# A fused decoder block on one core: the ways into and out of the seven-product down projection

## The chip, the core and the metric

One Trainium2 chip, one core. The time is that of one execution on the device, in microseconds; a measurement is the median of several runs.

## The reference, cut to what matters

The kernel computes one decoder block on 2048 tokens of width 1024 in float32: an input projection, two kinds of mixers, an output projection, and a SwiGLU feed-forward of width 2816. The change touches only the end of it:

```
u = rmsnorm(h, ln2_g)
h = h + (silu(u @ w_gate) * (u @ w_up)) @ w_down
out = rmsnorm(h, final_g)
```

## The kernel before

**Number format.** Every float32 matmul is made of three: each operand is split into a high part (a copy by ScalarE, type fp32r) and a low part (raw minus high, by the vector engine), and high x high, high x low and low x high are added in a PSUM bank.

**Seven products.** The feed-forward works on pairs of 512-token blocks, p = 0 and 1 (`NPAIR` = 2). Each 2 x 2 block product is done as seven products of sums of blocks in place of eight (Strassen's way, in Winograd's form). In the gate and up stage the operands made from u are `B11, B21, T2, T1, T3, B22, T4`, each 128 x 2048, and the weights `A11, A12, S2, S1, S3, S4, A22`, in that order, for `NG` = 22 groups (even groups are gate, odd ones up; `NJ` = 11 pairs of groups). A product is 12 matmuls of 128x512. In `ffn(p)` the vector engine combines and multiplies into `au[0..3]` (the four blocks of the activated result) and then makes three sums of them, in `gq[1..3]`: `s1 = au2 + au1` (line 2050), `s2 = s1 - au0` (2052), `s4 = au3 - s2` (2062). SyncE (SP), which issues all DMAs in program order, stores the four blocks (`store_a`, line 629) and the three sums (`store_s`, 634) to a scratch in HBM. `gq[0..3]` also hold the gate's results before that: the last readers are lines 2024, 2038, 2048 and 2058.

**The down projection.** `down(p)` has 7 products of `NJ` = 11 rows, `NR` = 77 ring rows. A ring row is 128 x 1024: one half from `w_down` or its combined form `t_scr`, one half from the stored blocks (`load_row`, lines 668 and 675). It goes through a ring of `CRING` = 4 slots; the slot of row rr is free when row rr-4 is done (`s_row`). ScalarE splits high (`row_hi`, 1566), the vector engine low (`row_lo`, 2110), each two rows ahead in its program, and TensorE does 12 matmuls (1165 to 1167). Ring slot 3 lies on `gq`: its high part on gq[0] and gq[1], its raw and low part on gq[2] and gq[3]. So `load_row` for rr = 3 waits until all sums are stored (`s_sst >= 48 * NJ * (p + 1)`), and it is called only at the start of SP's `down(p)`, behind all stores of the last group; rows 0 to 2 are loaded within the last group of `ffn(p)`.

**What goes on beside the rows.** After each product the vector engine adds the four banks to the residual (`residual`, 2123), one per row at the first four rows of the next product. ScalarE sums the squares of finished halves (`out_square`, 1576; it waits for the residual add); for the last of them before the end it does so at product 6, rows j = 0 to 3, that is ring rows 66 to 69, behind `row_hi` of two rows ahead. Then come `out_sums` (2130), `out_root` (1583, with a table load), `out_rn` (2134), four `out_scale` (2139) at j = 5 to 8, and the stores of the outputs (`store_out`, 693; the first is waited for before the rest is issued). The second half of a pair's outputs follows after the last row: in pair 0 within the next gate stage, in pair 1 at the very end. The third and fourth weight block of the next gate stage wait for one and for four of these stores (lines 1500 and 1502), as their buffers held residuals.

**Preparing the next pair in down(0).** The operand pieces of pair 1 and the residual pieces are loaded one beside each ring row by the list `PIECES` (operands by name, `("r", n)` residuals), from row 4 on. `COMBINE_AT` gives the rows at which the vector engine makes T3, T1, T2, T4 (`combine`, 1959), `SPLIT_AT` the rows of the operand splits: `op_hi` (1481) on ScalarE one row earlier, `op_lo` (1991) on the vector engine. Counting semaphores (`s_ophi`, `s_oplo`) assume an order, so far that of the operand numbers.

**Combined weights.** In `ffn(0)` the combined down weights are made: `load_t(j)` (642) from group `T_LOAD` = 10 on, `t_step` (2095 to 2105, four adds) one group later, `store_t(j)` (647) two groups later, 1 MB each way, in the two buffers `tw`; the last is stored after the last group. The buffers were `h_last` before, so the first load waits for the store of u (`store_u`).

Of the kernel before, what the change touches and what calls it, by code (L numbers as in the profile page):

```python
# [40 lines left out]
P = 128  # L41
# [38 lines left out]
OPERAND_NAMES = {"B11": B11, "B21": B21, "T2": T2, "T1": T1, "T3": T3, "B22": B22, "T4": T4}  # L80
KH = 4
# [8 lines left out]
PIECES = (("r", 0), "T3", "T1", ("r", 2), "T2", ("r", 1), "T4", "B11", "B21", ("r", 3), "B22")  # L90
COMBINE_AT = {27: 0, 38: 1, 41: 2, 49: 3}
SPLIT_AT = {51: "B11", 54: "B21", 59: "T2", 61: "T1", 63: "T3", 70: "B22", 75: "T4"}
T_LOAD = 10
# [37 lines left out]
def block_program(nc, x, ln1_g, w_in, lb_logits, hgrn_norm_g, attn_sinks, attn_norm_g, w_out, ln2_g,  # L131
# [37 lines left out]
    with ExitStack() as ctx:  # L169
# [153 lines left out]
        dump = acc_last  # L323
        tw = [at(f"tw{i}", (P, 2, D), kk_at + 8 * K * i) for i in range(2)]

# [223 lines left out]
        def _(sp):  # L549
# [81 lines left out]
            def store_s(p, j, n):  # L631

                sp.wait_ge(s_au, 7 * (p * NJ + j) + (4, 5, 7)[n])
                sp.dma_start(a_scr[p, (3, 2, 5)[n], j, :, :], gq[1 + n][:, :]).then_inc(s_sst, 16)
# [14 lines left out]
            def load_row(p, rr):  # L649
# [12 lines left out]
                elif rr == 3:  # L662
                    sp.wait_ge(s_sst, 48 * NJ * (p + 1))
# [13 lines left out]
            def load_res(p, m, b, half):  # L677
                if half == m == 0 and b == 0:
# [5 lines left out]
                    if p:  # L684
                        sp.wait_ge(s_fo, 32 * TB * p)
                it = 2 * p + m
# [48 lines left out]
            def ffn(p):  # L735
# [5 lines left out]
                for g in range(NG):  # L741
                    j = g // 2
                    if p == 0 and g >= T_LOAD + 2:
# [6 lines left out]
                    else:  # L750
# [9 lines left out]
                        if last:  # L760
                            load_row(p, 1)
                            load_row(p, 2)
                        store_s(p, j, 0)
# [4 lines left out]
                    if p == 0 and g == 9:  # L768
                        store_u(NSB - 1, 0)
                        store_u(NSB - 1, 1)  # L770
                if p == 0:
                    store_t(NJ - 1)

            def down(p):
# [3 lines left out]
                for rr in range(3, NR):  # L778
# [47 lines left out]
        def _(pe):  # L826
# [280 lines left out]
            def ffn_product(p, g, o):  # L1107
# [6 lines left out]
                if g == 0:  # L1114
                    pe.wait_ge(s_oplo, PRODUCTS * p + o + 1)
# [76 lines left out]
        def _(act):  # L1192
# [392 lines left out]
            def down(p):  # L1585
                for rr in range(NR):
# [7 lines left out]
                    if q == 6 and j < TB:  # L1594
                        out_square(p, 2 * TB + j)
                    if q == 6 and j == TB + 1:
# [37 lines left out]
        def _(dve):  # L1634
# [350 lines left out]
            def op_lo(p, o):  # L1985

                dve.wait_ge(s_ophi, PRODUCTS * p + o + 1)
# [15 lines left out]
            def ffn(p):  # L2003
                for g in range(NG):
# [3 lines left out]
                    for o in range(PRODUCTS):  # L2008
# [30 lines left out]
                        if o == S4:  # L2039
# [5 lines left out]
                            if up:  # L2045
# [4 lines left out]
                                V.tensor_tensor(gq[1][:, :], au[2][:, :], au[1][:, :], ALU.add).then_inc(s_au, 1)  # L2050
                                dve.wait_ge(s_au, 7 * j + 4)
                                V.tensor_tensor(gq[2][:, :], gq[1][:, :], au[0][:, :], ALU.subtract).then_inc(s_au, 1)
                        if o == A22 and up:
# [8 lines left out]
                            V.tensor_tensor(gq[3][:, :], au[3][:, :], gq[2][:, :], ALU.subtract).then_inc(s_au, 1)  # L2062
# [79 lines left out]
            def down(p):  # L2142
                for rr in range(NR):
# [5 lines left out]
                    if q == 6 and j == TB:  # L2149
# [193 lines left out]
```

## Time and profile before

| | us |
|---|---|
| median of 3 runs | 2281.8 |
| lowest, highest | 2279.1, 2285.85 |
| profiled execution, its own time | 2285.81 |
| its span, first to last instruction | 2284.0 |
| TensorE busy | 2222.6 (97%) |
| vector engine busy | 1438.3 (63%) |
| ScalarE busy | 1010.2 (44%) |
| GpSimd busy | 443.8 (19%) |

The profiled execution is a single one, 4 us above the median. Engines: PE is TensorE's matmuls, DVE the vector engine, ACT ScalarE, POOL GpSimd, SPq the queue of SyncE, which issues the DMAs. Starts are in us from the span's start. A bracket at the end of a row gives the idle time of that engine just before the instruction and what released it. TensorE's granted clock is told as a share of full speed: 1.00 is 2.4 GHz, 0.50 is 1.2 GHz. The first `ffn` ends at 1408 us, `down(0)` lasts to 1632 us, the second `ffn` to 2053 us.

### The profile page before, as it was taken

The numbers are of one execution on the slowest core, as the hardware profiler recorded it, in microseconds if no ns is written. First come the engines' busy times: TensorE is split into PE (matmuls) and PEld (weight loads), VectorE is DVE, ScalarE is ACT, GpSimd is POOL, SyncE is SP. The second block draws the span as 40 slices with busy tenths as digits, with TensorE's granted clock in tenths as the row PEclk, the third lists the DMA queues.
The fourth block names the chain that finished last, engine by engine and source line by source line (L and its number), as shares of the span: only waits on it lengthen the run. The fifth ranks groups of instructions, "written<-read, shape, count | busy, mean of one in ns | idle before, by whom it ended". The sixth has DMA issues, their size and how long they took to land.

```text
span 2284.0 us, 29991 instructions
## 1 busy us (share of the span) xinstructions
PE 2222.6 (97%) x11144; PEld 1848.9 (81%) x11144; DVE 1438.3 (63%) x2170; ACT 1010.2 (44%) x1723; POOL 443.8 (19%) x344
## 2 busy tenths in 40 slices
PE   7999999999999999999999999999999999999997
PEld 6888878887888788878888887888788888887886
DVE  5775568656865677675566666467665555554555
ACT  5554455445554554444433333345533333333444
POOL 2231022201220122032233331000232222210000
PEclk9999999999999999999999999999999999999999
DMA  4222333233233313533345656788443232326765
GB/s 122 92 75 80 115 102 96 90 107 105 81 121 97 111 58 119 194 105 117 116 164 183 223 205 216 255 269 262 149 137 108 99 109 98 110 89 213 229 221 197
DMA packets 260705, 321.80 MB, mean 141 GB/s; under 512 B 17233, under 2 KB 168785, under 8 KB 259537
## 3 DMA queue, kind: packets, MB, share of 16 engines
q1 hardware_dynamic: 258256, 311.50, 41.5%
q10 hardware_dynamic: 2304, 8.39, 0.9%
q8 instruction: 89, 1.46, 0.3%
q14 instruction: 56, 0.45, 0.1%
HBM read 242.76 MB, written 77.07 MB: 140 GB/s over the span
## 4 chain that ended last, share of the span: by engine, by line
PE 86%; DVE 5%; issue 3%; ACT 3%; DMA 2%; POOL 0%; SPq 0%; ACTq 0%; DVEq 0%; POOLq 0%
PE M L1138 9%; PE M L1140 9%; PE M L1139 9%; PE M L831 7%; PE M L833 7%; PE M L832 7%; PE M L1165 3%; PE M L1167 3%; PE M L1166 3%; PE X L1165 3%; PE X L1166 3%; PE X L1167 3%; PE X L1140 3%; PE X L1139 3%; PE X L1138 3%
## 5 line engine op out<-in xcount | busy, mean ns | idle before, releaser
L2110 DVE TENSOR_TENSOR ring_lo<-ring_raw,ring_hi 128x1024 fp32r<-128x1024 f32 x154 | 189.4, 1230 | 186.9 <-ACT ring_hi L1566 186.5
L1663 DVE TENSOR_TENSOR wlo<-raw,whi 128x1024 fp32r<-128x1024 f32 x120 | 152.0, 1267 | 230.3 <-ACT whi L1201 230.1
L831 PE MATMUL M<-uhi,whi 128*128 128x512 f32 (+1 forms) x720 | 286.4, 398 | 3.7 <-DVE wlo L1663 2.1
L833 PE MATMUL M<-uhi,wlo 128*128 128x512 f32 (+1 forms) x720 | 278.7, 387 | 0.0
L832 PE MATMUL M<-ulo,whi 128*128 128x512 f32 (+1 forms) x720 | 278.1, 386 | 0.0
L1566 ACT ACTIVATE ring_hi<-ring_raw 128x1024 fp32r<-128x1024 f32 x154 | 162.8, 1059 | 239.4 <-DMA ring_raw<-a_scr 236.2
L1138 PE MATMUL M<-t_hi,wu_hi 128*128 128x512 f32 x616 | 240.8, 391 | 4.1 <-DVE gq L2032 2.3
L1140 PE MATMUL M<-t_hi,wu_lo 128*128 128x512 f32 x616 | 240.6, 391 | 0.0
L1139 PE MATMUL M<-t_lo,wu_hi 128*128 128x512 f32 x616 | 240.4, 390 | 0.0
L1201 ACT ACTIVATE whi<-raw 128x1024 fp32r<-128x1024 f32 x120 | 126.6, 1055 | 196.9 <-PE M L833 146.2
L2000 DVE TENSOR_TENSOR wu_lo<-fraw,wu_hi 128x512 fp32r<-128x512 f32 x132 | 127.5, 974 | 120.3 <-ACT wu_hi L1507 120.0
L2254 POOL TENSOR_TENSOR pr<-pr,rd 128x512 f32<-128x512 f32 x64 | 84.4, 1318 | 539.7 <-DVE rd L1696 539.7
L831 PEld LDWEIGHTS M<-uhi,whi 128*128 128x128 f32 x720 | 136.9, 190 | 32.3 <-issue 4.2
L833 PEld LDWEIGHTS M<-uhi,wlo 128*128 128x128 f32 x720 | 136.4, 189 | 27.9
L2306 POOL TENSOR_TENSOR fs<-fraw 128x512 f32<-128x512 f32 x44 | 64.8, 1474 | 481.1 <-DMA fraw<-in_w_gate_dram 214.9
L832 PEld LDWEIGHTS M<-ulo,whi 128*128 128x128 f32 x720 | 137.1, 190 | 24.3
L1138 PEld LDWEIGHTS M<-t_hi,wu_hi 128*128 128x128 f32 x616 | 115.9, 188 | 29.8 <-DVE wu_lo L2000 5.6
L1165 PE MATMUL M<-ring_hi 128*128 128x512 f32 x308 | 123.1, 400 | 15.4 <-DVE ring_lo L2110 15.4
L1139 PEld LDWEIGHTS M<-t_lo,wu_hi 128*128 128x128 f32 x616 | 116.1, 188 | 24.1
L1140 PEld LDWEIGHTS M<-t_hi,wu_lo 128*128 128x128 f32 x616 | 116.0, 188 | 24.1
L2312 POOL TENSOR_TENSOR fraw<-fraw,fs 128x512 f32<-128x512 f32 x44 | 57.4, 1305 | 372.1 <-DVE wl_lo L2000 372.0
L1277 ACT ACTIVATE pr<-pr,nm 128x256 f32<-128x256 f32 x128 | 64.2, 502 | 145.0 <-DVE nms L1722 145.0
(277 smaller groups left out, 5109.3 us busy)
## 6 DMA issues: line engine op xcount, KB each, us to landing
raw<-in_w_in_dram SPq DMA_DIRECT2D x88, 512.0 KB, 3.8
ring_raw<-a_scr SPq DMA_DIRECT2D x154, 256.0 KB, 3.6
fraw<-in_w_gate_dram SPq DMA_DIRECT2D x44, 512.0 KB, 4.6
fraw<-in_w_up_dram SPq DMA_DIRECT2D x44, 512.0 KB, 4.8
a_scr<-au SPq DMA_DIRECT2D x88, 256.0 KB, 2.3
ring_raw<-t_scr SPq DMA_DIRECT2D x88, 256.0 KB, 3.0
a_scr<-gq SPq DMA_DIRECT2D x66, 256.0 KB, 2.5
ring_raw<-in_w_down_dram SPq DMA_DIRECT2D x66, 256.0 KB, 3.0
```

The source lines that it names most:

```text
L831: mm(bank, whi[s][:, kb, :], hi, start=first, stop=False)
L832: mm(bank, whi[s][:, kb, :], lo, start=False, stop=False)
L833: return mm(bank, wlo[s][:, kb, :], hi, start=False, stop=last)
L1138: mm(bank[:, :], wh[:, k, :], hi[:, k, :], start=start and k == 0, stop=False, skip_group_check=True)
L1139: mm(bank[:, :], wh[:, k, :], lo[:, k, :], start=False, stop=False, skip_group_check=True)
L1140: last = mm(bank[:, :], wl[:, k, :], hi[:, k, :], start=False, stop=k == KH - 1, skip_group_check=True)
L1165: mm(banks[b][:, :], hi[:, 1, tokens], hi[:, 0, :], start=first, stop=False, skip_group_check=True)
L1166: mm(banks[b][:, :], hi[:, 1, tokens], lo[:, 0, :], start=False, stop=False, skip_group_check=True)
L1167: done = mm(banks[b][:, :], lo[:, 1, tokens], hi[:, 0, :], start=False, stop=last, skip_group_check=True)
L1566: A(hi[:, :, :], raw_r[:, :, :], ACT.Copy).then_inc(s_rowhi, 1)
L1663: V.tensor_tensor(wlo[s][:, :, :], raw[s][:, :, :], whi[s][:, :, :].bitcast(F32), ALU.subtract).then_inc(s_lo[s], 1)
L2110: V.tensor_tensor(lo[:, :, :], raw_r[:, :, :], hi[:, :, :].bitcast(F32), ALU.subtract).then_inc(s_rowlo, 1)
```

## The change

Four edits, all in the second half of the kernel.

1. The sums of the last group of each `ffn(p)` go to three buffers of their own, `sx`, which lie on the second `tw` buffer (and on parts of the second half's residuals). The vector engine waits before the first of them: in pair 0 for the store of combined weights 9, in pair 1 for all outputs of pair 0. `load_row` for rr = 3 moves into the last group, ahead of the stores of the sums, and waits for the last reader of gq (`s_c21[1]`) and for the sums of the groups before. The wait for all sums moves to the first residual load of the second half.
2. In `down(p)` the squares of product 6 come at j = 2 to 5 in place of 0 to 3, and what follows from them two rows later: `out_sums` at j = 6, `out_root` and `out_rn` at 7, the scalings at 7 to 10.
3. The operands are split in another order, all of them by row 65, and B22's pieces are loaded before the last residual's. `SPLIT_ORDER` gives the counters the place of each operand.
4. `T_LOAD` is 9 in place of 10, the last `store_t` goes to the start of group 21, and the store of u goes to the end of group 8.

```diff
+SPLIT_ORDER = (tuple(range(PRODUCTS)), (B11, T2, T1, T3, B21, T4, B22))
-PIECES = (("r", 0), "T3", "T1", ("r", 2), "T2", ("r", 1), "T4", "B11", "B21", ("r", 3), "B22")
-COMBINE_AT = {27: 0, 38: 1, 41: 2, 49: 3}
-SPLIT_AT = {51: "B11", 54: "B21", 59: "T2", 61: "T1", 63: "T3", 70: "B22", 75: "T4"}
-T_LOAD = 10
+PIECES = (("r", 0), "T3", "T1", ("r", 2), "T2", ("r", 1), "T4", "B11", "B21", "B22", ("r", 3))
+COMBINE_AT = {27: 0, 37: 1, 39: 2, 48: 3}
+SPLIT_AT = {50: "B11", 52: "T2", 54: "T1", 59: "T3", 61: "B21", 63: "T4", 65: "B22"}
+T_LOAD = 9
...
+        sx = [at(f"sx{i}", (P, T), kk_at + 8 * K + 2 * K * i) for i in range(3)]
+        def sums_of(j):
+            return sx if j == NJ - 1 else gq[1:4]
...
-                sp.dma_start(a_scr[p, (3, 2, 5)[n], j, :, :], gq[1 + n][:, :]).then_inc(s_sst, 16)
+                sp.dma_start(a_scr[p, (3, 2, 5)[n], j, :, :], sums_of(j)[n][:, :]).then_inc(s_sst, 16)
...
                 elif rr == 3:
-                    sp.wait_ge(s_sst, 48 * NJ * (p + 1))
+                    sp.wait_ge(s_c21[1], NJ * (p + 1))
+                    sp.wait_ge(s_sst, 48 * (NJ * (p + 1) - 1))
...
+                if m and b == 0:
+                    sp.wait_ge(s_sst, 48 * NJ * (p + 1))
...
-                    if p == 0 and g >= T_LOAD + 2:
+                    if p == 0 and 0 <= g - T_LOAD - 2 < NJ:
                         store_t(g - T_LOAD - 2)
...
                             load_row(p, 1)
                             load_row(p, 2)
+                            load_row(p, 3)
                         store_s(p, j, 0)
...
-                    if p == 0 and g == 9:
+                    if p == 0 and g == T_LOAD - 1:
                         store_u(NSB - 1, 0)
                         store_u(NSB - 1, 1)
-                if p == 0:
-                    store_t(NJ - 1)
...
-                for rr in range(3, NR):
+                for rr in range(CRING, NR):
                     load_row(p, rr)
...
-                    pe.wait_ge(s_oplo, PRODUCTS * p + o + 1)
+                    pe.wait_ge(s_oplo, PRODUCTS * p + SPLIT_ORDER[p].index(o) + 1)
...
-                    if q == 6 and j < TB:
-                        out_square(p, 2 * TB + j)
-                    if q == 6 and j == TB + 1:
+                    if q == 6 and 2 <= j < 2 + TB:
+                        out_square(p, 2 * TB + j - 2)
+                    if q == 6 and j == TB + 3:
                         out_root(p, 0)
...
-                dve.wait_ge(s_ophi, PRODUCTS * p + o + 1)
+                dve.wait_ge(s_ophi, PRODUCTS * p + SPLIT_ORDER[p].index(o) + 1)
...
-                                V.tensor_tensor(gq[1][:, :], au[2][:, :], au[1][:, :], ALU.add).then_inc(s_au, 1)
+                                if g == NG - 1 and p:
+                                    dve.wait_ge(s_fo, 32 * TB * p)
+                                elif g == NG - 1:
+                                    dve.wait_ge(s_ts, 16 * (NJ - 1))
+                                s1, s2, _ = sums_of(g // 2)
+                                V.tensor_tensor(s1[:, :], au[2][:, :], au[1][:, :], ALU.add).then_inc(s_au, 1)
                                 dve.wait_ge(s_au, 7 * j + 4)
-                                V.tensor_tensor(gq[2][:, :], gq[1][:, :], au[0][:, :], ALU.subtract).then_inc(s_au, 1)
+                                V.tensor_tensor(s2[:, :], s1[:, :], au[0][:, :], ALU.subtract).then_inc(s_au, 1)
...
-                            V.tensor_tensor(gq[3][:, :], au[3][:, :], gq[2][:, :], ALU.subtract).then_inc(s_au, 1)
+                            _, s2, s4 = sums_of(g // 2)
+                            V.tensor_tensor(s4[:, :], au[3][:, :], s2[:, :], ALU.subtract).then_inc(s_au, 1)
...
-                    if q == 6 and j == TB:
+                    if q == 6 and j == TB + 2:
                         out_sums(p, 0)
-                    if q == 6 and j == TB + 1:
+                    if q == 6 and j == TB + 3:
                         out_rn(p, 0)
-                    if q == 6 and 0 <= j - TB - 1 < TB:
-                        out_scale(p, 0, j - TB - 1)
+                    if q == 6 and 0 <= j - TB - 3 < TB:
+                        out_scale(p, 0, j - TB - 3)
```

## Rows read from the trace of the kernel before

**Rows 1.** The page: engine totals, instruction groups, DMA issues (last column: us to landing).

```profile
PE 2222.6 (97%) x11144; PEld 1848.9 (81%) x11144; DVE 1438.3 (63%) x2170; ACT 1010.2 (44%) x1723; POOL 443.8 (19%) x344
...
L2110 DVE TENSOR_TENSOR ring_lo<-ring_raw,ring_hi 128x1024 fp32r<-128x1024 f32 x154 | 189.4, 1230 | 186.9 <-ACT ring_hi L1566 186.5
...
L1165 PE MATMUL M<-ring_hi 128*128 128x512 f32 x308 | 123.1, 400 | 15.4 <-DVE ring_lo L2110 15.4
...
ring_raw<-a_scr SPq DMA_DIRECT2D x154, 256.0 KB, 3.6
```

**Rows 2.** Stretches: length, busy us of five engines, clock, DMA share, GB/s.

```profile
1420.00:1422.00 2.00, 0.35 (x1) 0.35 (x2) 1.56 (x2) 1.39 (x2) 0.00 (x0) 0.50 0.99 354
1500.00:1600.00 100.00, 100.00 (x440) 82.03 (x439) 69.50 (x58) 52.19 (x58) 0.00 (x0) 1.00 0.82 265
```

**Rows 3.** Timeline of TensorE: rows 0, 1, 3, 4 of down(0), and its successor.

```profile
1408.07 0.39 PE L1165 MATMUL M<-ring_hi 128*128 128x512 f32 x1
...
1411.50 0.50 PE L1165 MATMUL M<-ring_hi 128*128 128x512 f32 x1 [0.55 <-DVE ring_lo L2110]
...
1421.65 0.79 PE L1165 MATMUL M<-ring_hi 128*128 128x512 f32 x1 [4.38 <-DVE ring_lo L2110]
...
1426.70 0.39 PE L1165 MATMUL M<-ring_hi 128*128 128x512 f32 x1
...
1632.36 0.39 PE L1138 MATMUL M<-b_hi,wl_hi 128*128 128x512 f32 x1
```

**Rows 4.** Timeline of SyncE's queue, way into down(0): last sum's store, row 3's load.

```profile
1410.59 0.43 SPq L634 DMA_DIRECT2D a_scr<-gq  x1
...
1414.27 0.33 SPq L668 DMA_DIRECT2D ring_raw<-in_w_down_dram  x1
```

**Rows 5.** Timeline of TensorE: rows 0, 3 and 4 of down(1).

```profile
2053.13 0.39 PE L1165 MATMUL M<-ring_hi 128*128 128x512 f32 x1
...
2067.33 0.80 PE L1165 MATMUL M<-ring_hi 128*128 128x512 f32 x1 [5.03 <-DVE ring_lo L2110]
...
2072.13 0.39 PE L1165 MATMUL M<-ring_hi 128*128 128x512 f32 x1
```

**Rows 6.** Timelines of three engines, way into down(1): row 2's load and split.

```profile
2051.70 0.43 SPq L675 DMA_DIRECT2D ring_raw<-a_scr  x1
...
2053.39 0.68 DVE L2058 TENSOR_TENSOR au<-M,gq 128x512 f32<-128x512 f32 x1
...
2056.92 1.06 ACT L1566 ACTIVATE ring_hi<-ring_raw 128x1024 fp32r<-128x1024 f32 x1 [2.16 <-DMA ring_raw<-a_scr]
```

**Rows 7.** Timeline of TensorE: rows 69 to 72 of down(0).

```profile
1604.09 0.39 PE L1165 MATMUL M<-ring_hi 128*128 128x512 f32 x1
...
1608.08 0.50 PE L1165 MATMUL M<-ring_hi 128*128 128x512 f32 x1 [1.10 <-DVE ring_lo L2110]
...
1611.64 0.50 PE L1165 MATMUL M<-ring_hi 128*128 128x512 f32 x1 [0.51 <-DVE ring_lo L2110]
...
1616.99 0.50 PE L1165 MATMUL M<-ring_hi 128*128 128x512 f32 x1 [2.30 <-DVE ring_lo L2110]
```

**Rows 8.** Timelines of the vector engine and ScalarE at the same place.

```profile
1605.88 2.14 DVE L2110 TENSOR_TENSOR ring_lo<-ring_raw,ring_hi 128x1024 fp32r<-128x1024 f32 x1 [1.74 <-ACT ring_hi L1566]
...
1608.65 0.63 ACT L1576 ACTIVATE acc_last<-res 128x512 f32<-128x512 f32 x1 [2.81 <-DVE res L2123]
...
1612.84 1.90 ACT L1481 ACTIVATE b_hi<-b_raw 128x2048 fp32r<-128x2048 f32 x1
```

**Rows 9.** Waits of TensorE, 2230 to 2284 us: total, times, longest.

```profile
PE M L1165 <- DVE ring_lo L2110: 1.1, 2, 0.6
```

**Rows 10.** Tail of down(1): timeline of the vector engine; waits of SyncE's queue, 2236 to 2284 us.

```profile
2268.53 1.28 DVE L2139 SCALAR_TENSOR_TENSOR res<-res,rnrm,gfrow 128x1024 f32<-128x1024 f32 x1
2270.95 0.69 DVE L2123 TENSOR_TENSOR res<-res,M 128x512 f32<-128x512 f32 x1 [1.14 <-PE M L1167]
...
SPq L693 <- DMA out_dram<-res: 3.4, 1, 3.4
```

## The prediction

> **What bounds the kernel now.** I read the page first. TensorE is busy 2222.6 us [rows 1] of a span of 2284.0, so at most 61.4 us of idle time can go, and the busy part only where its clock was down. The page's largest idle sum in front of a matmul of the second half is 15.4 us, before line 1165, the down projection, and its releaser is the vector engine's low split of a ring row (line 2110). Then the table of stretches [rows 2]: in mid-stream the down projection has TensorE busy 100% at the full granted clock (1.00, the 2.4 GHz level), and at 1420 to 1422 us it is almost idle at 0.50, the 1.2 GHz level. So the loss sits where a down projection begins and ends, and I read those places in order of time.
>
> A ring row is 12 matmuls. Undisturbed, row starts are 2.72 us apart, so 77 rows would take 209.5 us. The first down projection takes 1408.07 to 1632.36 [rows 3] = 224.3 us, 14.8 us more.
>
> **Way in, first pair.** Row 1 starts at 1411.50 where 1410.79 was due (1408.07 + 2.72): 0.7 us late, and the clock stays up. Rows 1 and 2 take it to 1416.94, but row 3 starts at 1421.65, 4.7 us late, and row 4 comes 5.05 us later in place of 2.72, since the clock is down: 2.3 us more [rows 3]. Why is row 3 late? SyncE (SP) issues the first of its two loads at 1414.27, having waited for the last store of a sum (line 634, issued at 1410.59) to land, and only then can the row travel and be split [rows 4]. Its buffer, ring slot 3, is the memory of gq, whose sums are being stored.
>
> **Way in, second pair.** The same: row 0 starts at 2053.13, row 3 at 2067.33 with 5.03 us idle before it, so it was due at about 2062.15 (an end of a matmul reaches 0.16 us past the next start), and row 4 at 2072.13 [rows 5]. That is 5.2 us of waiting and 2.1 us of low clock.
>
> **Part 1, sums apart and row 3 loaded in advance.** The three sums of the last group go to sx. What slot 3 then waits for is the multiply of line 2058, the last reader of gq[3], begun at 2053.39 and 0.68 us long [rows 6]. So the pair is issued at about 2054.15 and 2054.6 instead of behind the landed stores. The time of such a load from the second issue to landing has a median of 3.6 us on the page [rows 1]; row 2 of this pair, issued at 2051.70 and taken by ScalarE at 2056.92, needed 5.2 us [rows 6]. High and low split take 1.06 us [rows 6] and 1.23 us [rows 1], with hand-overs 2.35 us. Row 3 is then ready between 2060.6 and 2062.2, and due at 2062.15: 0 to 0.1 us late. I take 0. In the first pair line 2058 lies equally far behind the start of row 0, so the same holds.
>
> What it pushes back: row 3's two loads now stand on SP ahead of the five remaining stores, which go out some 1.3 us later than before. Nobody reads them before row 22, 60 us later, and the residual loads behind them have as long. Behind the stores comes row 4: five issues of 0.43 us [rows 4] with their gaps take some 2.3 us (2055.1 to 2057.4), then its own pair, second issue 2057.8, landing after 3.6 to 5.2 us, ready 2063.8 to 2065.4, due 2064.87: 0 to 0.5 us late. I take 0.3 us for each way in; a delay that short left the clock up at 1411.50 [rows 3]. The Trainium skill ("DMA: Bandwidth & Descriptors", section on queues, rings and completion order) says that an engine's semaphore increment lands only after every earlier write of that engine. By it row 3 would be independent of the stores behind it and row 4 would wait out the 1.25 MB ahead of it. No row shows the two apart; by it the sum would keep row 3 at 0 and put row 4 at its late end, 0.4 us less gain in all.
>
> The vector engine's new waits ask for stores finished long before (combined weights of step 9, a whole group earlier; the first pair's outputs): 0. If step 9's store were still under way, the wait would hold the rest of the last group. The early load gains 4.7 + 2.3 + 5.2 + 2.1 = 14.3 us, less 0.6 = 13.7.
>
> **Part 2, way out: squares two rows later.** In the first pair row starts go 1604.09, 1608.08, 1611.64, 1616.99 [rows 7], the end being 1632.36 [rows 3]. Eight rows are 21.8 us; they take 28.3: 6.5 us lost. ScalarE's square waits for the residual add, the add stands behind the vector engine's low split, and that stands behind ScalarE's high split, which is queued behind the previous square: at 1608.65 ScalarE had been idle 2.81 us for a residual [rows 8]. High split, low split, residual, square make a ring of 3.56 us a row (1608.08 to 1611.64) against 2.72. Then at 1612.84 comes the 1.90 us split of B22 on ScalarE, and the next row is 2.6 us late with 1.8 us of low clock behind it. Two rows later every square finds its residual done, so the ring opens; B22 goes to row 65. In the second pair there is no B22: two waits for a low split, 1.1 us together [rows 9], that is two rows of 3.56 us, 1.7 us lost.
>
> I take all of it back, 8.2 us. One delay in it has another cause: the low split at 1605.88 took 2.14 us instead of 1.23 [rows 8] while GpSimd was making sums, and that stays. Outside the ring a row has three rows' time, 8.2 us, from the release of its slot: less 0.8 for two issues, 3.6 for landing and 2.35 for the splits that leaves 1.4 us, so 0.9 more is covered; if it is not, 0 to 1 us stays. Nothing excludes that.
>
> **Part 3, splits in another order.** The same seven ScalarE splits (1.90 us, as at 1612.84) and seven vector splits, none added. Rows 59 to 63 keep every second place; row 65 takes the fourth. ScalarE then has 1.0 + 1.9 us in a 2.72 us row once, and less in the next. Each operand's last piece is loaded at least three rows before its split. 0, with 0 to 1 us for the range. SP issues no DMA more; B22's pieces and the last residual's change places.
>
> **Part 4, T_LOAD a step earlier.** The 1 MB load and store of each step move one group forward. The last group of the first pair loses four vector adds of 0.68 us, which lie in front of its sums: row 1 comes up to 0.1 us sooner. The 1 MB store also leaves SP at 1411, where it preceded row 3. The two u stores wait on SP before group 9 instead of 10; what is behind them is not due for a group. 0.
>
> **Part 5, what gets later: outputs.** The scalings of the first half of a pair's outputs move to rows 73 to 76. In the last pair they now run up against the residual adds after the last row. The last scaling began at 2268.53, right behind the low split of row 76 (1.14 us from start to start, so 2267.4), the first add at 2270.95, and ScalarE's four squares and the end follow that add [rows 10]. With the split at 2267.1 to 2267.4 and three scalings of 1.22 us behind it, the add begins at 2271.9 to 2272.2: **1.0 us lost**, between 0.9 and 1.3. After the first pair the third and fourth weight blocks of the next gate stage wait for those outputs to be stored (lines 1500, 1502). Four stores, the first alone and waited for 3.4 us [rows 10], are down 3.6 us after the last row; block four must be on ScalarE by 6.8 us after it (three products of 2.72 less two splits). 0, with 3 us of slack.
>
> **Sum.** 13.7 + 8.2 - 1.0 = 20.9, less 0.5 for small delays of the unbounded kind above = 20.4 us. The profiled execution took 2285.8 us (span 2284.0), so 2265.4 by its own time; the median shown, 2281.8, is 4.0 lower, so I predict 2281.8 - 20.4 = **2261.4 us**.
>
> **Rivals.** (A) The wait on row 3 is replaced by one on DMA: rows 3 and 4 stay late by 1 to 2 us each way in and the clock falls once more. Row 2's 5.2 us speaks for it [rows 6], the 2.7 us of stores and the free row ahead against. It keeps about 3 us for each way in: gain 14.4, 2267.4. Chance 0.16. (B) The way out is bound by loads or by GpSimd's sharing and not by the ring, so half of the 8.2 stays, or the fourth split in a row costs it again: gain 16 with a part of A, down to 13, about 2267. The 2.14 us split speaks for it, the idle 2.81 us with releaser "residual" against. Chance 0.12. (C) Slower: the output stores come so late that ScalarE stands at line 1502 and TensorE starves at the fourth product. Each us beyond 6.8 costs one; it turns the sign only when they land 24 us later than I work out (3.2 slack and 20.4 gain), then 2285 or more. Four stores of 3.4 us one after another, from 5 us before the last row's end, would be down 8.6 us after it and cost 1.8. Chance 0.02. (D) The change does not do what it says: row 3 still waits for a landed store (of the group before) or the squares still meet a fresh residual. The waits' counts speak against; gain under 8, 2276. Chance 0.03.
>
> **Numbers.** Forecast 0.67. Its own range is 2257 to 2265: no more than the 22.5 us found can go, runs scatter by 3 us. To hold 8 in 10 with A and B the upper end goes to 2270. 0.3%, 6.8 us, is what a measurement can tell from no change: faster 0.95, same 0.03, slower 0.02.
>
> **What would show it.** Row 3 of each pair starting within 0.5 us of 2.72 us after row 2 at clock 1.00, ScalarE's wait before it under 3 us, no row start over 2.9 us apart in the last ten rows, first add of the tail 1 us closer to the last matmul. Wrong if TensorE's time in a down projection stays above 215 us, if a gap appears at the fourth product of the second gate stage, or a new one near rows 50 to 65.

## The result, and the profile after

| | before | after |
|---|---|---|
| median of 5 runs, us | 2284.6 | 2268.6 |
| lowest, highest | 2279.1, 2285.85 | 2267.18, 2272.28 |
| profiled execution | 2285.81 | 2272.28 |
| its span | 2284.0 | 2270.6 |
| first down projection, row 0 to the next stage | 224.3 | 214.2 |
| second down projection, row 0 to its last matmul's end* | 219.6 | 214.8 |
| last matmul's end to the end of the span | 11.3 | 12.3 |

(*) The end of a matmul is taken here as its start plus 0.23 us, the distance of two matmuls at full clock.

The ratio after to before is 0.9937 (0.9923 to 0.9951): faster by 14 us, the medians differ by 16. The median lies 7.2 us above the forecast of 2261.4, outside the forecast's own range of 2257 to 2265 and inside the one that was widened to 2270 for the rivals. Two thirds to four fifths of the forecast gain of 20.4 us came. The kernel before has a median of 2284.6 over five runs, where the forecast started from 2281.8 over three; set on the same base the forecast would have been 2264.2, and the miss 4.4 us.

The page of the kernel after (the lines that answer to [rows 1]; line numbers moved, 1165 is 1174, 2110 is 2125):

```profile
PE 2217.9 (98%) x11144; PEld 1847.1 (81%) x11144; DVE 1437.9 (63%) x2170; ACT 1010.0 (44%) x1723; POOL 445.8 (20%) x344
...
L1174 PE MATMUL M<-ring_hi 128*128 128x512 f32 x308 | 120.7, 392 | 6.1 <-DVE ring_lo L2125 6.1
```

Idle time in front of the down projection's matmuls fell from 15.4 to 6.1 us, and some busy time went too, since less of it ran at the low clock. What is left is in the ways in. Timeline of TensorE, both ways in of the kernel after (start, length, engine, line, operation):

```profile
1408.57 0.39 PE L1174 MATMUL M<-ring_hi 128*128 128x512 f32 x1
...
1411.90 0.50 PE L1174 MATMUL M<-ring_hi 128*128 128x512 f32 x1 [0.45 <-DVE ring_lo L2125]
...
1422.28 0.50 PE L1174 MATMUL M<-ring_hi 128*128 128x512 f32 x1 [1.90 <-DVE ring_lo L2125]
...
2043.50 0.39 PE L1174 MATMUL M<-ring_hi 128*128 128x512 f32 x1
...
2052.57 0.50 PE L1174 MATMUL M<-ring_hi 128*128 128x512 f32 x1
...
2058.02 0.50 PE L1174 MATMUL M<-ring_hi 128*128 128x512 f32 x1 [2.44 <-DVE ring_lo L2125]
2058.89 0.63 PE L1174 MATMUL X<-ring_hi 128*128 128x512 f32 x1
```

Row 3 starts at 2052.57 without a wait: where [rows 5] had 5.03 us of idle time there is 0.1 us of delay. But the next row, row 4, waits, 1.90 us in the first pair (2.1 us late, start to start) and 2.44 us in the second (2.7 us late), and there the clock falls once more: seven matmuls behind it start 0.43 us apart in place of 0.23. The wait has moved by one row and is about half as long.

Why row 4 is late, from SyncE's queue and from ScalarE in the second pair. Line 675 loads the weight half of a row, 682 the activation half, 640 and 635 are the stores of sums and blocks:

```profile
2044.47 0.33 SPq L675 DMA_DIRECT2D ring_raw<-in_w_down_dram  x1
2044.85 0.43 SPq L682 DMA_DIRECT2D ring_raw<-a_scr  x1
2045.33 0.90 SPq L640 DMA_DIRECT2D a_scr<-sx  x2
2046.27 1.66 SPq L635 DMA_DIRECT2D a_scr<-au  x2
2047.98 0.60 SPq L640 DMA_DIRECT2D a_scr<-sx  x1
2048.63 0.60 SPq L675 DMA_DIRECT2D ring_raw<-in_w_down_dram  x1
2049.27 0.67 SPq L682 DMA_DIRECT2D ring_raw<-a_scr  x1
```

```profile
2050.19 1.06 ACT L1575 ACTIVATE ring_hi<-ring_raw 128x1024 fp32r<-128x1024 f32 x1 [2.52 <-DMA ring_raw<-a_scr]
2055.65 1.06 ACT L1575 ACTIVATE ring_hi<-ring_raw 128x1024 fp32r<-128x1024 f32 x1 [4.40 <-DMA ring_raw<-a_scr]
```

Row 3 is issued at 2044.47, as soon as the last reader of gq (line 2058 before, 2072 now) is done, and is with ScalarE 5.3 us after its second issue. Behind it go the five stores. Their issues stretch (two of them take 1.66 us where one takes 0.43), so row 4's second issue is at 2049.27, 5.8 us after row 0's start instead of the 4.7 I had; and the row is with ScalarE 6.4 us later, where I had allowed 3.6 to 5.2. In the first pair the same two numbers are 5.6 and 5.7 us. Stretches of the same time (length, busy us of five engines, clock, DMA share, GB/s):

```profile
2044.00:2048.00 4.00, 3.55 (x16) 2.62 (x15) 3.07 (x5) 2.12 (x2) 0.00 (x0) 1.00 0.74 235
2048.00:2052.00 4.00, 4.00 (x20) 3.27 (x18) 1.65 (x2) 1.06 (x1) 0.00 (x0) 1.00 1.05 362
2052.00:2056.00 4.00, 3.58 (x15) 2.36 (x13) 0.51 (x1) 0.35 (x1) 0.00 (x0) 1.00 1.00 345
```

From 2048 to 2056 the 16 DMA engines are busy all the time (mean share 1.00 to 1.05). I read this as transfers that wait for their turn behind other bytes, and not for their own latency; the stretches alone do not show it.

The way out is clean. ScalarE at the place of [rows 8]: every square (1585) stands directly behind a high split (1575) and waits for nothing, and what the high splits wait for is their load:

```profile
1602.34 1.06 ACT L1575 ACTIVATE ring_hi<-ring_raw 128x1024 fp32r<-128x1024 f32 x1 [1.31 <-DMA ring_raw<-a_scr]
1603.30 0.61 ACT L1585 ACTIVATE acc_last<-res 128x512 f32<-128x512 f32 x1
...
1605.11 1.06 ACT L1575 ACTIVATE ring_hi<-ring_raw 128x1024 fp32r<-128x1024 f32 x1 [1.10 <-DMA ring_raw<-a_scr]
1606.07 0.62 ACT L1585 ACTIVATE acc_last<-res 128x512 f32<-128x512 f32 x1
```

A slow low split that runs beside GpSimd's sums is there still, 1.85 us at 1603.43 in place of 1.23, and costs nothing (that GpSimd is what slows it was not tested):

```profile
1603.43 1.85 DVE L2125 TENSOR_TENSOR ring_lo<-ring_raw,ring_hi 128x1024 fp32r<-128x1024 f32 x1 [1.16 <-ACT ring_hi L1575]
```

The tail pays for it. Vector engine after the last low split, where [rows 10] had 1.14 us of idle time before the first add:

```profile
2253.86 3.67 DVE L2154 SCALAR_TENSOR_TENSOR res<-res,rnrm,gfrow 128x1024 f32<-128x1024 f32 x3
2257.45 0.68 DVE L2138 TENSOR_TENSOR res<-res,M 128x512 f32<-128x512 f32 x1
```

The last matmul ends at 2258.33; the first add begins 0.9 us before that, where it began 1.8 us before it.

### The profile page after: what moved, and what is told of

It is laid out like the page before. It is cut to its first block, busy times and chain, and to the rows that moved or that the text cites. A ratio compares the mean times of both kernels' runs of the same rounds, so it can differ in the third digit from the quotient of the medians.

```text
span 2270.6 us, 29999 instructions
## 1 busy us (share of the span) xinstructions
PE 2217.9 (98%) x11144; PEld 1847.1 (81%) x11144; DVE 1437.9 (63%) x2170; ACT 1010.0 (44%) x1723; POOL 445.8 (20%) x344
## 4 chain that ended last, share of the span: by engine, by line
PE 87%; DVE 5%; issue 3%; ACT 2%; DMA 2%; SPq 0%; POOL 0%; ACTq 0%; DVEq 0%; POOLq 0%
PE M L1147 9%; PE M L1149 9%; PE M L1148 9%; PE M L840 7%; PE M L842 7%; PE M L841 7%; PE M L1174 3%; PE M L1176 3%; PE M L1175 3%; PE X L1149 3%; PE X L1147 3%; PE X L1148 3%; PE X L1175 3%; PE X L1174 3%; PE X L1176 3%
```

## The experiments

Eleven measurements, each set against the kernel before on the same chip: nine new kernels, one of them twice, and the changed kernel once more. Two theories of the late row 4: **S**, it waits out what stands ahead of it in SyncE's queue (the five stores, 1.25 MB); **R**, it shares the DMA engines with what is issued behind it. "Down 1" and "down 2" are the two down projections in the profiled execution, measured as in the table above, "row 4" the idle time of TensorE before that row, "tail" the time from the last matmul's end to the end of the span.

| kernel | median us | ratio to before, 95% | down 1, down 2 | row 4, both pairs | tail |
|---|---|---|---|---|---|
| after | 2268.6 | 0.9937 (0.9923, 0.9951) | 214.2, 214.8 | 1.90, 2.44 | 12.3 |
| changed_again | 2268.8 | 0.9933 (0.9920, 0.9946) | 213.4, 212.2 | 2.25, 1.59 | 12.2 |
| stores_beside_rows | 2261.4 | 0.9904 (0.9887, 0.9921) | 211.5, 210.7 | none | 12.3 |
| stores_beside_again | 2262.9 | 0.9905 (0.9890, 0.9920) | 212.5, 211.4 | none | 12.2 |
| residual_loads_later | 2268.1 | 0.9931 (0.9914, 0.9947) | 213.5, 212.4 | 1.47, 1.40 | 12.3 |
| stores_behind_row4 | 2268.2 | 0.9924 (0.9910, 0.9938) | 212.8, 212.3 | none (row 5: 1.41, 1.50) | 12.2 |
| t_load_back | 2269.1 | 0.9932 (0.9918, 0.9946) | 216.7, 212.7 | 3.81, 1.93 | 12.2 |
| squares_back | 2271.5 | 0.9949 (0.9934, 0.9964) | 216.3, 214.7 | 1.37, 2.33 | 11.4 |
| split_order_back | 2268.1 | 0.9934 (0.9920, 0.9949) | 214.6, 212.6 | 2.24, 1.96 | 12.3 |
| squares_alone | 2276.0 | 0.9958 (0.9945, 0.9972) | 219.3, 218.3 | row 3: 4.83, 4.99 | 12.1 |
| stores_tail | 2264.4 | 0.9910 (0.9896, 0.9924) | 211.6, 211.0 | none | 11.4 |
| stores_in_free_rows | 2262.4 | 0.9906 (0.9892, 0.9921) | 211.8, 210.2 | none | 11.4 |

**stores_beside_rows.** The stores leave the space between rows 3 and 4:

```diff
                         if last:
                             load_row(p, 3)
-                        store_s(p, j, 0)
-                        store_s(p, j, 1)
-                        store_a(p, j, 2)
-                        store_a(p, j, 3)
-                        store_s(p, j, 2)
+                        if not last:
+                            for n in range(5):
+                                store_rest(p, j, n)
...
                     load_row(p, rr)
+                    if rr in (5, 6, 7, 8, 9):
+                        for n in range(5):
+                            if (5, 6, 7, 8, 9)[n] == rr:
+                                store_rest(p, NJ - 1, n)
```

(`store_rest` issues the five in the old order.)

> The changed kernel, with the five stores that stand on SyncE between the loads of row 3 and row 4 issued one by one beside rows 5 to 9 instead. In the changed kernel's profile row 3 was in time in both ways in, and row 4 was the late one (1.9 and 2.4 us idle before it, once with the clock down behind it); its down projections took 214.2 and 214.8 us. Theory S (row 4 waits out the 1.25 MB of stores ahead of it in the queue): row 4 starts less than 0.3 us late in both, the clock stays at 1.00, the projections take about 212 and 210.5 us, and the time falls by 4 to 6 us against the changed kernel, to about 0.9915 of the kernel before. Theory R (row 4 shares the engines with the residual pieces and rows 5 and 6 behind it): row 4 stays 1.5 to 2.5 us late, no change of time beyond 1 us.

Row 4 has no wait in either pair, no projection is over 211.5 us, and the median is 7 us lower than the changed kernel's in the table at the top (5.9 us where the two were measured side by side, see below). This is theory S as written, at the upper end of the 4 to 6 us expected or a little above. Its queue (row 4) and ScalarE (rows 3 and 4) in the second pair, where row 0 starts at 2038.69:

```profile
2041.61 0.33 SPq L680 DMA_DIRECT2D ring_raw<-in_w_down_dram  x1
2041.99 0.47 SPq L687 DMA_DIRECT2D ring_raw<-a_scr  x1
```

```profile
2044.36 1.06 ACT L1582 ACTIVATE ring_hi<-ring_raw 128x1024 fp32r<-128x1024 f32 x1 [1.73 <-DMA ring_raw<-a_scr]
2046.25 1.06 ACT L1582 ACTIVATE ring_hi<-ring_raw 128x1024 fp32r<-128x1024 f32 x1 [0.82 <-DMA ring_raw<-a_scr]
```

Two things improve together: the second issue is 3.3 us after row 0's start instead of 5.8, and the row is with ScalarE 4.3 us later instead of 6.4. The two shares, 2.5 us of later issue and 2.1 us of longer travel, are about equal. Row 3 gains too: without the five stores behind it it is with ScalarE 4.3 us after its second issue, where it took 5.3 us with them in the kernel after. Over the profiles of all kernels that load row 3 in advance it is 3.8 to 4.8 us without the stores directly behind row 3 and 4.9 to 5.6 us with them. So stores behind a load do delay it, by about 0.9 us on average; row 3 has just that much to spare.

**residual_loads_later.** The pieces of residual 0, beside rows 4, 5, 6 and 8, go beside rows 7 to 10:

```diff
+                for rr in (4, 5, 6, 8):
+                    del pieces[rr]
...
+                    if 7 <= rr < 7 + TB:
+                        load_res(p, 0, rr - 7, 0)
```

> The changed kernel, with the four pieces of the first residual (256 KB each, beside rows 4, 5, 6 and 8) loaded beside rows 7 to 10; the five stores stay where they are. Theory S (the stores ahead hold row 4): row 4 is still 1.5 us late or more in at least one way in, time within 2 us of the changed kernel. Theory R (what is issued behind row 4 holds it): row 4 less than 0.5 us late in both, and 4 to 6 us less time.

Row 4 still waits 1.47 and 1.40 us (its start is 1.8 and 1.7 us late), and the time is the same. The bound for S was a start 1.5 us late or more, so S holds, narrowly. The waits are shorter than in the two profiles of the changed kernel (1.59 to 2.44), but squares_back, whose way in is the same, has one of 1.37 us. So what is issued behind row 4 is not the cause as a whole, and a share of some tenths of a microsecond is possible but not shown here.

**stores_behind_row4.** The same bytes in another order:

```diff
                             load_row(p, 3)
+                            load_row(p, 4)
                         store_s(p, j, 0)
...
                 for rr in range(CRING, NR):
-                    load_row(p, rr)
+                    if rr > CRING:
+                        load_row(p, rr)
```

> The changed kernel with the loads of row 4 between row 3's and the five stores. SyncE then waits for row 0 to be done before the stores go out, some 2 us later than now; the same bytes, another order. Theory S: row 4 is in time in both ways in (wait under 0.3 us). The 1.25 MB are now ahead of row 5, which is issued about 7 us after row 0 begins and must land by 11.8: with 3.1 us of stores it is 0 to 1.5 us late. Time 2 to 5 us below the changed kernel. Theory R (row 4 shares with what is issued behind it): row 4 stays 1 us late or more, since the stores are then right behind it.

The sharpest of the runs. With the stores directly behind row 4 instead of ahead of it, row 4 does not wait, and row 5, which now has them ahead, does. ScalarE in the second pair (rows 4 and 5), and TensorE at row 5:

```profile
2048.62 1.06 ACT L1577 ACTIVATE ring_hi<-ring_raw 128x1024 fp32r<-128x1024 f32 x1 [0.59 <-DMA ring_raw<-a_scr]
2054.58 1.06 ACT L1577 ACTIVATE ring_hi<-ring_raw 128x1024 fp32r<-128x1024 f32 x1 [4.90 <-DMA ring_raw<-a_scr]
```

```profile
2056.95 0.50 PE L1176 MATMUL M<-ring_hi 128*128 128x512 f32 x1 [1.50 <-DVE ring_lo L2127]
```

R falls as the cause of the wait: it wanted row 4 late with the stores right behind it. Row 5 also tells in what form the stores ahead cost time: its second issue comes 8.6 and 9.1 us after row 0's start, where stores_beside_rows has 6.8, but from there it takes 5.0 and 4.5 us, against 4.7 and 4.6. Its delay is time in SyncE's program, with hardly any longer travel. For row 4 of the changed kernel, where both grew, no run separates the two. The time did not fall by the 2 to 5 us expected in the medians (2268.2), since row 5's wait took row 4's place; the ratio, 0.9924, is 0.1% lower than the changed kernel's, within the intervals.

**t_load_back.** Edit 4 undone, which puts the last 1 MB store of combined weights ahead of row 4 as well:

```diff
-T_LOAD = 9
+T_LOAD = 10
...
+                if p == 0:
+                    store_t(NJ - 1)
```

> The changed kernel with edit 4 alone undone: T_LOAD 10, and the last 1 MB store of combined weights at the start of SyncE's program for the down projection, now behind the five stores and ahead of row 4. Theory S (row 4 waits out the bytes ahead of it): 1 MB more is 2.5 us at the 410 GB/s that the stretches show, so in the first pair row 4 is 4 to 5 us late instead of 2.1 and the clock falls to 0.50 behind it (2 us more): the first down projection takes 218 to 219 us instead of 214.2, the second is unchanged at 212.5 to 215, and the time is 4 us above the changed kernel. Rival (the load of row 4 is late for its own latency, whatever is ahead): both unchanged, time the same within 1 us.

Row 4 of the first pair waits 3.81 us (4.0 us late, start to start) with low clock behind it, the second pair, where this edit changes nothing, waits 1.93 us. First pair, SyncE (the store, then row 4) and ScalarE:

```profile
1411.80 0.72 SPq L653 DMA_DIRECT2D t_scr<-tw  x1
1412.57 0.68 SPq L675 DMA_DIRECT2D ring_raw<-in_w_down_dram  x1
1413.29 1.19 SPq L682 DMA_DIRECT2D ring_raw<-a_scr  x1
```

```profile
1420.18 1.06 ACT L1576 ACTIVATE ring_hi<-ring_raw 128x1024 fp32r<-128x1024 f32 x1 [5.91 <-DMA ring_raw<-a_scr]
```

More bytes ahead, a later row: the dose goes the way S says, with 1.9 us for 1 MB rather than 2.5. The down projection takes 216.7 us, less than the 218 to 219 expected, and the median shows only 0.5 us. So edit 4 is worth some 2.5 us in the profile, which the runs' scatter does not confirm.

**squares_back.** Edit 2 undone, the rest as changed:

```diff
-                    if q == 6 and 2 <= j < 2 + TB:
-                        out_square(p, 2 * TB + j - 2)
-                    if q == 6 and j == TB + 3:
+                    if q == 6 and 0 <= j < 0 + TB:
+                        out_square(p, 2 * TB + j - 0)
+                    if q == 6 and j == TB + 1:
                         out_root(p, 0)
```

(and `out_sums`, `out_rn` and `out_scale` two rows earlier likewise)

> The changed kernel with edit 2 alone undone: the squares of product 6 at rows 66 to 69 again, sums, root and scalings two rows earlier; the order of the splits stays new. Ring theory (high split, low split, residual add and square wait for each other at 3.56 us a row): the first down projection loses 2 to 4 us near rows 69 to 72, without the 2.6 us of the B22 split, the second 1.7 us with two waits of about 0.55 us; the tail is 1.0 us shorter (11.3 us from the last matmul to the end instead of 12.3). In all 3 to 5 us slower than the changed kernel. Rival (the way out was lost to the split of B22 alone): no gap at rows 69 to 72, 1 us faster than the changed kernel by the tail.

Three waits come back in the first way out, and two of 0.51 and 0.55 us in the second. TensorE in the first:

```profile
1601.29 0.50 PE L1174 MATMUL M<-ring_hi 128*128 128x512 f32 x1 [0.90 <-DVE ring_lo L2125]
1604.85 0.50 PE L1174 MATMUL M<-ring_hi 128*128 128x512 f32 x1 [0.55 <-DVE ring_lo L2125]
1608.41 0.50 PE L1174 MATMUL M<-ring_hi 128*128 128x512 f32 x1 [0.53 <-DVE ring_lo L2125]
```

The row starts are 3.56 us apart, as in [rows 7], and ScalarE is again released by the residual add:

```profile
1597.95 0.63 ACT L1585 ACTIVATE acc_last<-res 128x512 f32<-128x512 f32 x1 [1.89 <-DVE res L2138]
1598.49 0.19 ACT L1585 ACTIVATION_READ_ACCUMULATOR acc_last<-res 128x1 f32 x1
1598.58 1.04 ACT L1575 ACTIVATE ring_hi<-ring_raw 128x1024 fp32r<-128x1024 f32 x1
```

The tail is 0.9 us shorter. The median is 2.9 us higher, at the lower end of the 3 to 5 us expected, and the intervals of the two ratios overlap: what carries this run is the profile. There the ring theory holds; the rival, that B22 alone was to blame, would have shown no gap. By row starts the ring takes 3.0 us in the first way out and 1.8 in the second. Before, the first way out lost 6.5: so B22's split, while it stood inside the ring, added some 3.5 us.

Of the clock: row 4 of the second pair waits 2.33 us here and TensorE's granted clock stays up behind it, while it fell behind the 2.30 us wait of [rows 7]. TensorE at this wait:

```profile
2057.10 0.50 PE L1174 MATMUL M<-ring_hi 128*128 128x512 f32 x1 [2.33 <-DVE ring_lo L2125]
```

The next row starts 2.85 us later, and the clock is 1.00 from 2058 to 2059. Before, it was 0.50 from 1618 to 1619, and the row took 4.45 us.

**split_order_back.** Edit 3 undone, that is `SPLIT_ORDER[1]`, `PIECES`, `COMBINE_AT` and `SPLIT_AT` as before:

```diff
-SPLIT_AT = {50: "B11", 52: "T2", 54: "T1", 59: "T3", 61: "B21", 63: "T4", 65: "B22"}
+SPLIT_AT = {51: "B11", 54: "B21", 59: "T2", 61: "T1", 63: "T3", 70: "B22", 75: "T4"}
```

> The changed kernel with edit 3 alone undone: operands split in the old order, B22 at row 70 and T4 at row 75, the last residual loaded before B22; squares stay at rows 68 to 71. Theory N (the squares' ring was what made the way out late, and the order of the splits is worth nothing by itself): at row 70 ScalarE has 1.06 + 0.82 + 1.90 us in a row of 2.72, which the lead of 1.4 us covers, so the first down projection stays within 1 us of 214.2, and the three small waits (0.24 to 0.33 us at 1550 to 1582) go: time the same within 1 us. Rival O (the B22 split so late costs 2.6 us and the clock, as before): 2 to 5 us slower, with a wait over 1 us near row 72.

No wait at all in the way out, and the same time. B22's split stands between two squares and the next high split catches up within a row:

```profile
1603.00 0.61 ACT L1585 ACTIVATE acc_last<-res 128x512 f32<-128x512 f32 x1
...
1603.61 1.91 ACT L1490 ACTIVATE b_hi<-b_raw 128x2048 fp32r<-128x2048 f32 x1
1605.42 1.04 ACT L1575 ACTIVATE ring_hi<-ring_raw 128x1024 fp32r<-128x1024 f32 x1
```

One part of my expectation missed: small waits did not go, they stand elsewhere (0.23 and 0.35 us, at 1463 and 1535 us). They stand in other places in each profile, and nothing ties them to the order.

**squares_alone.** The kernel before with edit 2 alone (the diff of edit 2 in the change).

> The kernel before with edit 2 alone: squares at rows 68 to 71, sums, root and scalings two rows later; the rest as before (B22 split at row 70, T4 at 75, row 3 loaded behind the stores). Ring theory: the way out gives back all of its 8.2 us and the tail costs 1.0: the first down projection takes 217 to 218.5 us instead of 224.3, the second 217.5 to 218.5 instead of 219.6, tail 12.3; gain 7 us, ratio 0.997. Rival (the late B22 split is needed for the loss to go): the first down projection keeps 2 to 4 us at row 72, gain 3 to 5 us.

No wait in either way out, with B22 still at row 70, so here too the rival falls. The first projection takes 219.3 us, 0.8 more than my upper bound: its way in lost 0.3 us more than before, and about 1 us went in two small waits (0.18 and 0.30 us, at 1552 and 1555) and the starts behind them. Row 3 behind the landed stores:

```profile
1419.06 0.80 PE L1165 MATMUL M<-ring_hi 128*128 128x512 f32 x1 [4.83 <-DVE ring_lo L2110]
```

The ratio, 0.9958, is 9.6 us, at the upper side of the 7 expected (6.4 to 12.6 by its interval). By the ratios edit 2 alone brings two thirds of what the whole change does, by the medians (8.5 of 16.0) half; the intervals leave room for both.

**stores_tail.** stores_beside_rows with the squares at rows 67 to 70 and what follows one row earlier than in the change.

```diff
-                    if q == 6 and 2 <= j < 2 + TB:
-                        out_square(p, 2 * TB + j - 2)
+                    if q == 6 and 1 <= j < 1 + TB:
+                        out_square(p, 2 * TB + j - 1)
```

> The kernel with the five stores beside rows 5 to 9, and besides the squares of product 6 at rows 67 to 70, sums at 71, root and scalings one row earlier (72 to 75). Ring theory: one row of distance is enough, since a square then waits for a residual add of the row before; the last scaling ends before the first add after the last row, so the tail from the last matmul to the end is 11.3 us again instead of 12.3, and no wait appears at rows 68 to 74: 1 us less than the kernel with the stores moved, 2260.5 us. Rival: one row is too little, the ring closes again and 1 to 3 us come back in each way out: 2262 to 2265 us.

In the profile it is as the ring theory has it: tail 11.4, no wait in the last ten rows of either projection; the first add after the last scaling has idle time before it again:

```profile
2243.04 2.48 DVE L2161 SCALAR_TENSOR_TENSOR res<-res,rnrm,gfrow 128x1024 f32<-128x1024 f32 x2
2245.95 0.69 DVE L2145 TENSOR_TENSOR res<-res,M 128x512 f32<-128x512 f32 x1 [0.43 <-PE M L1183]
```

The times do not show it (2264.4, not 2260.5; the intervals of the two kernels overlap almost wholly): 0.9 us is below what they resolve.

**changed_again, stores_beside_again, stores_in_free_rows.** The two main kernels side by side, and a third that has the stores beside rows that load nothing else, with the squares at rows 67 to 70 as in stores_tail:

```diff
-                    if rr in (5, 6, 7, 8, 9):
+                    if rr in (10, 13, 16, 7, 20):
```

> The changed kernel once more, beside the two others of this call, so that they are compared on one chip in the same rounds. Both theories: 2267 to 2270 us, row 4 late by 1.5 to 2.5 us in both ways in.

> The kernel with the five stores beside rows 5 to 9 once more. Theory S: 5 to 7 us below the changed kernel of the same call, ratio 0.990 to 0.991. If the first measurement was luck: 2 us or less below it.

> The stores one each beside rows that load nothing else (fourth block at 7, sums at 10, 13 and 20, third block at 16), and the squares at rows 67 to 70. If bytes ahead of a row are what makes it late, none is late here by more than 0.2 us, both down projections take 210.2 to 211 us, the tail 11.3: 1 to 2 us below the kernel with the stores beside rows 5 to 9. If that kernel has no wait left to remove, only the tail's 1 us shows, which five rounds can hardly tell.

Both first measurements repeat. Moving the stores gives 0.9905 against 0.9933, 5.9 us by medians. In the third the only waits left are row 1's, one in each way in. Waits of TensorE, 1400 to 1620 us and 2035 to 2251 us (total, times, longest):

```profile
PE M L1181 <- DVE ring_lo L2132: 0.5, 1, 0.5
...
PE M L1181 <- DVE ring_lo L2132: 0.5, 1, 0.5
```

Its second projection takes 210.2 us, 0.7 over 77 undisturbed rows; the first, 211.8, misses the 210.2 to 211 expected by small delays under any wait shown. By time it is level with stores_beside_again (2262.4 and 2262.9). Both lie about 6 us below the changed kernel and 20 below the kernel before; the order of the stores is the one improvement on the changed kernel that the times tell apart.

## Why the prediction was right and wrong

**What bounds the kernel: right.** The gain came from where a down projection begins and ends; the second gate stage between them took 420.8 us before and after.

**Part 1, row 3 early: right in mechanism, the size wrong by its second half.** Row 3 was 0.1 us late, as worked out. The step that failed is the bound on row 4: "landing after 3.6 to 5.2 us, ready 2063.8 to 2065.4, due 2064.87: 0 to 0.5 us late". It had two mistakes. I took the five issues at 0.43 us each; SyncE's issues stretched, and row 4 went out 0.9 and 1.1 us later than I had it. And I took the landing time from rows that did not stand behind such a group of stores (the median of the page, and row 2, with a store and row 1's loads in front of it), while row 4 had 1.25 MB of stores in front: it took 5.7 and 6.4 us. Together that is 2.1 and 2.7 us late in place of 0.3, plus 1.7 us at the low clock in the second pair (row 4's twelve matmuls take 4.4 us in place of 2.7). None of the signs that I had named looked at row 4. Those that stood for success all came: row 3 in time at full clock, no gap in the last ten rows, the first add 1 us closer to the last matmul. Of those that stood for failure one came in part: three waits of 0.24 to 0.33 us at rows 51, 53 and 62, which the second profile of the same kernel (changed_again) does not have. The term "14.3 us, less 0.6 = 13.7" measured about 8: before, the two projections together took 24.9 us more than undisturbed rows would; less the 8.2 of the ways out that is 16.7; in the profile after 10.0 are left, of which 1.3 are three small waits at 1550 to 1582 us, so 8.7. That is 8.0 us of gain.

The rule of the Trainium skill that I set beside it ("DMA: Bandwidth & Descriptors", on queues, rings and completion order) pointed the right way, and was priced too low, at 0.4 us. The traces agree with it for what stands ahead: row 4 waited with the stores ahead of it and not in stores_behind_row4. They agree less with my reading that row 3 would be independent of the stores behind it: it was in time, but landed about 0.9 us later with them. Rival A, with 0.16, is nearest to what came: row 4 late by 2 to 3 us each way in, the clock down in one, 2267.4 against 2268.6. Row 3, which A had late as well, was not. I had argued against A with the stores and the free row ahead of row 4, which the stretched issues and the longer travel used up.

**Part 2, the way out: right, 8.2 us.** No wait is left in the last ten rows of either projection (224.3 and 219.6 had 6.5 and 1.7 in them), the slow low split beside GpSimd is covered, and undoing or adding edit 2 alone moved the waits as the ring says, at 3.56 us a row in squares_back.

**Part 3, the order of the splits: right, 0, once the squares are moved.** With the squares two rows later it makes no difference where B22 stands (split_order_back, squares_alone). B22 cost time before only because it stood in the ring; with the squares left where they were, moving it alone would have been worth some 3.5 us (an estimate, from the 6.5 us lost before less the 3.0 in squares_back).

**Part 4, T_LOAD: the reason right, booked as 0.** "The 1 MB store also leaves SP at 1411, where it preceded row 3" is worth some 2.5 us of the first down projection (216.7 against 214.2) once row 4 is the late one. One profile shows it, the medians do not.

**Part 5, the tail: right.** 1.0 us predicted, 1.0 measured (11.3 to 12.3). The weights that wait for the output stores (lines 1500, 1502) cost TensorE nothing: from 1625 to 2040 us it has one wait for a weight split, 0.9 us, and the kernel before has the same one.

**The sum** was 20.4; by parts it came to 8.0 + 8.2 - 1.0, less 1.3 of small waits and 0.5 by which the first projection began later: 13.4 us, the difference of the two spans. Of both kernels the slowest of the five runs was the profiled one, and that of the kernel after lies further from its median, so the medians show 16. The one term explains most of the miss: with the stores moved, the gain by medians is 21.9 and 19.8 us in two measurements, against the 20.4 forecast. That the time of 2261.4 us came out to the tenth in one of them is chance, since the kernel before stood at 2283.3 us there and not at 2281.8.

## What to carry to other kernels

When a wait is removed, ask what the next transfer in the same queue has in front of it: count the bytes and the issues ahead of it, not the usual latency. Name a sign that would show the next transfer late, too. Stores that nobody reads soon belong behind the loads of a pipeline's first rows, or one by one beside later rows. And where two engines hand work to each other in turn, look for a cycle: one that is longer than the period costs its excess in every round, and a distance of one or two rounds opens it at no cost but a later end.

## What the runs showed of the hardware that I had not expected

Issues on SyncE stretch when many stand close together: two stores of 256 KB took 1.66 us at 2046.27, with the DMA engines at a share of about 0.8, against 0.90 us for the two before them; row 4's pair took 1.31 us at a share of 1.05, against 0.81 us for row 3's; a second issue that took 0.43 us elsewhere took 1.19 us in t_load_back. What stretches them no run shows; it is not only that all engines are busy. Order in the one queue decides who is late, almost to the row: the same 1.25 MB made row 4 wait when ahead of it and row 5 when one place later. The granted clock fell to 0.50 behind waits of 2.30 and 2.44 us and stayed at 1.00 behind waits of 2.25 (changed_again) and 2.33 us (squares_back), so about the same delay costs nothing more in one place and 1.7 us more in another.
